# Moving the conditioning's pieces further back in a weight stream, and a little closer together

## The reference

```python
def swiglu(x, w_gu, w_down):
    g, u = jnp.split(x @ w_gu, 2, axis=-1)
    return (jax.nn.silu(g) * u) @ w_down

def first_block(...):
        x = x + 0.5 * swiglu(rmsnorm(x, ffn1_norm[l]), ffn1_w_gu[l], ffn1_w_down[l])
...
def ada_terms(cond, w, b):
    return jnp.split(jax.nn.silu(cond) @ w + b, N_ADA, axis=-1)
```

## Time and profile before

| | |
|---|---|
| median of 3 runs | 890.19 us (889.85 to 890.60) |
| the profiled execution | 890.65 us, its span 888.9 us |
| TensorE busy | 878.5 us (99%) |
| VectorE busy | 631.6 us (71%) |
| ScalarE busy | 460.7 us (52%) |
| DMA, mean over the span | 242 GB/s |
| granted TensorE clock | full, 0.997 in the mean |
| the 48 pieces of the conditioning on VectorE | 58.3 us, 1214 ns each |

### The profile page before, as it was taken

How to read it: one execution, slowest core, us unless ns; L and a number is a source line. 1 busy time by engine, 2 the same in 40 slices (tenths; PEclk the granted TensorE clock), 3 DMA queues, 4 the chain that set the end, 5 groups by cost and what they waited for, 6 DMA issues and landing times.

```text
span 888.9 us, 11084 instructions
## 1 busy us (share of the span) xinstructions
PE 878.5 (99%) x4079; PEld 732.8 (82%) x4079; DVE 631.6 (71%) x883; ACT 460.7 (52%) x697; POOL 40.8 (5%) x66
## 2 busy tenths in 40 slices
PE   9999999999999999999999999999999999999996
PEld 7878888888998888888888888888888888888885
DVE  6769987837558877688578886875768766665743
ACT  6546554626688475446535554454445344444530
POOL 0010000022103000000000000001000100000000
PEclk9999999999999999999999999999999999999998
DMA  9899999774654454454699999975755577777741
GB/s 365 346 323 352 359 363 351 270 237 145 182 175 175 162 193 164 149 186 143 218 308 348 344 329 323 333 257 163 257 179 177 182 248 241 240 233 246 250 120 47
DMA packets 94879, 215.12 MB, mean 242 GB/s; under 512 B 14520, under 2 KB 46185, under 8 KB 94697
## 3 DMA queue, kind: packets, MB, share of 16 engines
q1 hardware_dynamic: 94104, 212.97, 69.8%
q10 hardware_dynamic: 720, 1.44, 0.4%
HBM read 204.66 MB, written 9.72 MB: 241 GB/s over the span
## 4 chain that ended last, share of the span: by engine, by line
PE 94%; DMA 2%; DVE 1%; issue 1%; ACT 1%; SPq 0%; POOL 0%; POOLq 0%; DVEq 0%
PE ps L741 29%; PE ps L743 29%; PE ps L742 29%; DMA t_raw<-in_f_up 2%; PE ps L679 1%; PE ps L656 1%; PE ps L649 1%; PE ps L858 1%; PE ps L874 1%; PE ps L816 0%; PE ps L850 0%; PE ps L798 0%; DVE t_wl L1209 0%; DMA t_acc<-in_xT 0%; PE ps L865 0%
## 5 line engine op out<-in xcount | busy, mean ns | idle before, releaser
L1209 DVE TENSOR_TENSOR t_wl<-t_raw,t_wh 128x1024 fp32r<-128x1024 f32 (+3 forms) x308 | 360.4, 1203 | 103.3 <-ACT t_wh L916 102.4
L916 ACT ACTIVATE t_wh<-t_raw 128x1024 fp32r<-128x1024 f32 (+3 forms) x308 | 307.8, 1040 | 106.9 <-DMA t_raw<-in_f_up 63.3
L741 PE MATMUL ps<-t_wh,t_XH 128*128 128x512 f32 (+2 forms) x640 | 250.2, 391 | 1.3 <-DVE t_wl L1209 1.3
L743 PE MATMUL ps<-t_wh,t_XL 128*128 128x512 f32 (+2 forms) x640 | 247.1, 386 | 0.0
L742 PE MATMUL ps<-t_wl,t_XH 128*128 128x512 f32 (+2 forms) x640 | 246.8, 386 | 0.0
L741 PEld LDWEIGHTS ps<-t_wh,t_XH 128*128 128x128 f32 x640 | 120.2, 188 | 24.8 <-DVE t_wl L1209 2.1
L743 PEld LDWEIGHTS ps<-t_wh,t_XL 128*128 128x128 f32 x640 | 120.1, 188 | 24.0
L742 PEld LDWEIGHTS ps<-t_wl,t_XH 128*128 128x128 f32 x640 | 120.3, 188 | 22.9
L741 PE MATMUL ps<-t_wh,t_YH 128*128 128x512 f32 x288 | 113.1, 393 | 0.2 <-DVE t_YL L1634 0.2
L743 PE MATMUL ps<-t_wh,t_YL 128*128 128x512 f32 x288 | 112.2, 390 | 0.0
L742 PE MATMUL ps<-t_wl,t_YH 128*128 128x512 f32 x288 | 112.2, 389 | 0.0
(11 more groups left out here) (225 smaller groups left out, 614.1 us busy)
## 6 DMA issues: line engine op xcount, KB each, us to landing
t_raw<-in_f_up SPq DMA_DIRECT2D x130, 512.0 KB, 5.6
t_raw<-in_f_dn SPq DMA_DIRECT2D x66, 512.0 KB, 5.5
t_raw<-in_ada SPq DMA_DIRECT2D x48, 512.0 KB, 6.3
inner_rows<-t_tp SPq DMA_DIRECT2D x60, 128.0 KB, 3.8
t_tp<-inner_rows SPq DMA_DIRECT2D x15, 512.0 KB, 5.2
t_raw<-in_mkv SPq DMA_DIRECT2D x8, 512.0 KB, 3.6
t_raw<-in_ga SPq DMA_DIRECT2D x8, 512.0 KB, 3.3
t_raw<-in_gc SPq DMA_DIRECT2D x8, 512.0 KB, 3.2
```

The lines of the kernel that those rows point to most:

```text
L741: pe.matmul(o, xh, h, start=k == 0, stop=False)
L743: x = pe.matmul(o, xl, h, start=False, stop=k == n - 1)
L916: act.activation(wh[:, m % SPL, lo:w], raw[:, n % RAW, lo:w], ACT.Copy).then_inc(hi_made, 1)
L1209: dve.tensor_tensor(wl[:, n % RAW, lo:w], raw[:, n % RAW, lo:w], wh[:, m % SPL, lo:w].bitcast(F32), ALU.subtract).then_inc(drained, 1)
```

## The change

It lets the first net's pieces begin at unit 18, the nineteenth, in place of unit 10, and places the 24 over 42 units in place of 50 (0.57 a unit in place of 0.48). The last one stands one unit later than before. The second net's pieces stand as before. The lines of everything below move by two.

```diff
--- before.py
+++ after.py
@@ -77,9 +77,11 @@
         while units and (units[0][0].startswith(tag + "_") if tag else units[0][0][:3] not in ("f2_",)):
             part.append(units.pop(0))
         ada = [("ada", i) for t in terms for i in range(8 * t, 8 * t + 8)]
+
+        start = 18 if tag == "f1" else 10
         for i, u in enumerate(part):
             out.append(u)
-            while ada and i >= 10 and (24 - len(ada)) * 50 < (i - 9) * 24:
+            while ada and i >= start and (24 - len(ada)) * (60 - start) < (i - start + 1) * 24:
                 out.append(ada.pop(0))
     assert not units
     return out
```

## The result

| | before | after |
|---|---|---|
| median | 890.33 us (889.85 to 890.60, 4 runs) | 897.38 us (894.69 to 897.65, 4 runs) |
| the profiled execution | 890.65 us, span 888.9 | 897.65 us, span 895.9 |
| TensorE busy | 878.5 us | 881.9 us |
| VectorE busy | 631.6 us | 631.6 us |
| granted TensorE clock, mean | 0.997 | 0.996 |

The change makes the kernel slower: ratio 1.0073, with an interval of 1.0053 to 1.0093. The engines do the same work; VectorE's busy time is equal to the digit. So the 7 us are waiting, and, for a part, matmuls that take longer: TensorE's busy time has grown by 3.4 us with no matmul added. Most of the rest stands behind the waits: at 61.70, for instance, the gap is 0.69 us, but TensorE has lost 0.96 us when its matmuls have their usual distance again. The like happens at seven places after the change and at two before.

A forecast was written before the change was run, and what follows sets the result against it. TensorE sets the pace, closely fed by VectorE and DMA from 60 to 120 us. The 6.0 us lost at unit 52, with 0.8 gained at unit 20 included, added to median 890.19 gave 896.2 us; range 889.0 to 898.2.

The forecast's parts named there:

- Before unit 19: Up to unit 20: first reload lands 1.25 us sooner, unit 19 in time, 0.9 us stall back, about 0.8 gained.
- One piece more in each round: Between block transposes from unit 19 on: 5, 4 and 5 pieces replace 4, 3 and 4, adding 1.14 us each round.
- The waits behind the reloads: VectorE idles 2.3, 1.9 and 1.8 us before splits 24, 32 and 40; block 4's transpose moves to 128.1.
- Where it is paid: Block 4's 7.0 us delay passes whole through block 5's relay to unit 52, which has 1.08 spare: 6.0 us lost.
- The stretch of 60 to 120 us: VectorE busy 58.9 of 60 us, DMA engines 97%: what stands here counts more than how early it starts.
- The stall goes and nothing takes its place: Rival: the 1.91 us stall before units 19 and 21 goes, nothing is added, 888.3 us; chance 0.15.
- Shorter relays when fewer transfers are on the way: Rival: relays below 8.5 us leave VectorE no idle time, giving 889.4 to 890.3 us; chance 0.20.
- Half of it: Rival: waits in only one or two rounds, or block 4's relay catches up; 892 to 893.5 us, chance 0.12.
- the rule that I weighed: Skill page's 2.0 us fixed plus bytes at 436 GB/s: a 7.6 us relay; the prediction trusted the trace's 10.7 to 11.0.

The follow-up runs named there:

- b: The changed kernel with VectorE working on 512 of each piece's 1024 columns, all transfers kept; 893.58 us, ratio 1.0029 to before.
- c: The changed kernel with VectorE working on 512 of each piece's 1024 columns and only those fetched; 889.56 us, ratio 0.9985 to before.
- d: The changed kernel with its start at unit 18 but its pieces spread over 46 units instead of 42; 892.69 us, ratio 1.0010 to before.
- e: The changed kernel's spacing (24 pieces over 42 units), but starting at unit 10 as before; 900.22 us, ratio 1.0101 to before.
- f_behind: The changed kernel with pieces 3, 7, 12 and 17 moved to stand first behind the reloads of blocks 1 to 4; 896.40 us, ratio 1.0064 to before.
- k_wait4: The kernel before, with TensorE held at unit 52 until the queue has passed four entries more; 895.27 us, ratio 1.0047 to before.
- k_wait3: The kernel before, with TensorE held at unit 52 until the queue has passed three entries more; 896.08 us, ratio 1.0046 to before.

## Why the prediction was right

The forecast was 896.2 us, in a range of 889.0 to 898.2; 897.38 was measured. Sign and stretch hold; the size came out near in part by luck, and the place where TensorE pays is wrong. By its own steps:

- **Before unit 19.** The first reload was put at 52.55, 1.25 us sooner; ScalarE sees it at 52.92, 0.88 sooner. Unit 19 is in time and unit 20 stalls for 0.69 us in place of the 0.9 forecast. Block 1's transpose was put at 57.9 and is at 58.15. This part is right within 0.3 us.
- **One piece more in each round.** Right: 3.55 us more of VectorE's work in three rounds, against 3 x 1.14. That VectorE's work and the bytes both matter is shown by b and c, that the spacing does by d.
- **The waits behind the reloads.** They are where I put them, before splits 24, 32 and 40, with 1.52, 0.79 and 2.01 us in place of 2.3, 1.9 and 1.8. I had taken the shortest relay that the trace of before shows, 10.7 us, as a floor for two of them; they took 9.9 and 9.6. The two rounds are 1 us shorter for it, the third is 0.5 longer than forecast. Block 4 is transposed at 126.91, not 128.1. As a cause of the loss these waits say less than I gave them: d's trace has them too, as long as after's, and is 3.1 us further behind than before, not 6.6. TensorE's waits sum to 4.9 us, just under the forecast's 5 to 8.
- **Where it is paid.** The step "the chain moves as a whole: 7.0 - 1.08 = 6.0 us lost at unit 52" failed. TensorE is 4.0 us behind at unit 47, less the 1.9 of before, and 6.8 at 48. The price is asked four units sooner, at unit 48, whose split waits for block 4's relay and then for block 5's transpose and for piece 17. I had followed unit 52's fetch alone and not asked what stands ahead of unit 48 in VectorE's list. Nor did the chain move as a whole: block 5's transpose comes 13.9 us behind block 4's, not 12.5. Unit 52's split is in time (it ends at 153.44, TensorE comes to it at 156.46).
- **A term that was missing.** The clock: 1.7 us behind the gap of 2.67. The sum had no term for it. That the forecast came out 1.2 us from the measured time is luck as far as this goes: the 1.1 us by which block 4 is sooner than forecast stands against it, and the run at 894.69, which the clock seems to have spared, is only 4.4 us above before. By the traces the 6.6 us are: -0.9 at unit 20, +3.0 at units 29 to 47, +2.8 at unit 48, +1.7 the clock.
- **The stretch of 60 to 120 us** was read rightly as the one that counts. But I read it as VectorE's; the earlier trace rows has two columns near full, and the other, the DMA share of 0.97, is as much of the cause. I priced a piece's 1.14 us in this stretch and never its 512 KB.

The rivals. *The stall goes and nothing takes its place* (888.3) would have needed the reload 6 us sooner; it came 0.9 sooner. *Shorter relays when fewer transfers are on the way*: two of the three were shorter, by 1 us, and none was under 8.5. *Half of it* (892 to 893.5) is where the median comes at 46 units.

On the rule that I weighed: the relays of blocks 1 to 5 in after and the other runs take 9.0 to 12.4 us; the shortest, 9.0, is from c_halfboth, where the transfers for the pieces are half as large (issue of the spill at 58.03, ScalarE's split of unit 24 at 67.07). The Trainium skill, page "DMA: Bandwidth & Descriptors", section "Anatomy of one DMA — SWDGE (gpsimd) path", has the figures from which the prediction made its estimate of 7.6 us for the three. No run comes under 9.0, even with less on the way, so the measurement decides; the transfers here are SyncE's, and the page's fit is for GpSimd's.

**What stays open.** How much of the transfers' part is bandwidth, and how much the order in SyncE's queue, was not separated. The DMA share fell, from 0.97 to 0.88, as the loss came: as I read it, the queue stands still with the relay and is then behind, but no run shows that by itself. Of after's four timed runs only one was traced; that the clock fell in two more and not in the one at 894.69 is read from their mean clocks. And why e is so far behind at unit 33 stays open.

## What to carry to other kernels

When the feeding engine and the transfers are both nearly full in a stretch (here 58.9 of 60 us, and a share of 0.97), ask of each operation added how many pass between the start of that stretch and each thing that the bound engine waits for, not how many there are in all; and price its bytes as well as its engine time. With the start at unit 18, one step of spacing (0.52 to 0.57 pieces a unit) went from 1 us to 7. And where a forecast makes a gap on TensorE of over 2 us, add what the clock may take behind it: here 1.7 us, by chance.

## What the runs showed of the hardware

- A single gap can cost more than it lasts. After gaps of 2.39, 2.67 and 3.15 us in a TensorE that was busy before, the granted clock was near one half for a while, 1.5 to 1.7 us of lost time; after gaps of 1.00, 1.51, 1.57, 1.78 (f_behind) and 2.61 us it stayed at 1.00. The length of the gap alone doesn't decide it, and one kernel has runs of either kind: four of k_wait4's six have a mean clock of 0.996, two of 0.998. The Trainium skill, page "TensorE: Matmul & The Clock Gate", section "Part 1: The HAM clock gate", says that the chip's own rhythm decides where a transition falls, not the kernel's; that fits 2.39 falling and 2.61 not, and no run here shows that rhythm.
- A relay through memory stayed long when less was on the way. Spill, reload and fetch of 512 KB each took 9.0 to 12.4 us for blocks 1 to 5 in all runs, and 9.0 to 10.8 with the pieces' transfers halved.
- A falling DMA share doesn't clear the transfers: it is 0.97 before and 0.88 after the change, and halving the pieces' transfers still gave 4 us.
- Single runs scatter more than most differences here: before had 889.8 to 890.6 in its first four and up to 893.4 in the 85 later ones, d_start18_46 890.2 to 894.1, k_wait3 892.5 to 898.1.
